# An RWKV-7 scan with two hops a chunk in place of three, in a hybrid decoder layer on one Trainium2 core

## The reference, cut to what matters

```
def step(s, inp):
    r_t, w_t, k_t, v_t, a_t, b_t = inp
    sa = jnp.einsum('bhij,bhj->bhi', s, a_t)
    s = s * w_t[:, :, None, :] + sa[..., None] * b_t[:, :, None, :] + v_t[..., None] * k_t[:, :, None, :]
    return s, jnp.einsum('bhij,bhj->bhi', s, r_t)
```

## Time and profile before

| | us |
|---|---|
| median of 3 runs | 4218.8 (4216.9 to 4219.01) |
| the profiled execution's own time | 4218.97 |
| its span | 4217.2 |
| TensorE busy | 3944.5 (94%) |
| VectorE busy | 2359.7 (56%) |
| ScalarE busy | 1541.6 (37%) |

### The profile page before, as it was taken

How to read it: one execution, slowest core, us unless ns; L and a number is a source line. 1 busy time by engine, 2 the same in 40 slices (tenths; PEclk the granted TensorE clock), 3 DMA queues, 4 the chain that set the end, 5 groups by cost and what they waited for, 6 DMA issues and landing times. The chain is left out here.

```text
span 4217.2 us, 85220 instructions
## 1 busy us (share of the span) xinstructions
PE 3944.5 (94%) x36213; PEld 3629.2 (86%) x36213; DVE 2359.7 (56%) x4632; ACT 1541.6 (37%) x2869; POOL 154.7 (4%) x152
## 2 busy tenths in 40 slices
PE   8999999999989999889978999969989899999998
PEld 4889999999988888889977777769869889999997
DVE  4445656332278886348877777545632464444446
ACT  3113232231177554334326666534411441111112
POOL 0000000000001111010000000000011000000000
PEclk9999999999999999999989999989998999999999
DMA  5323223233355554555641111042323031111112
GB/s 209 83 90 93 90 89 98 80 97 113 114 148 144 147 163 134 168 152 176 215 159 35 42 34 35 21 169 98 103 80 114 27 110 46 48 43 49 42 31 83
DMA packets 375321, 418.74 MB, mean 99 GB/s; under 512 B 50250, under 2 KB 317052, under 8 KB 374076
## 3 DMA queue, kind: packets, MB, share of 16 engines
q1 hardware_dynamic: 362703, 368.14, 28.6%
q0 software_dynamic: 7632, 27.84, 2.2%
q10 hardware_dynamic: 4608, 17.30, 1.0%
HBM read 289.10 MB, written 121.77 MB: 97 GB/s over the span
## 5 line engine op out<-in xcount | busy, mean ns | idle before, releaser
L245 PE MATMUL bank<-xn_hi,pw_whi 128*128 128x352 f32 (+1 forms) x2184 | 735.4, 337 | 20.6 <-PEq L54 8.8
L245 PE MATMUL bank<-xn_hi,pw_wlo 128*128 128x352 f32 (+1 forms) x2184 | 711.7, 326 | 0.0
L245 PE MATMUL bank<-xn_lo,pw_whi 128*128 128x352 f32 (+1 forms) x2184 | 711.3, 326 | 0.0
L245 PEld LDWEIGHTS bank<-xn_hi,pw_whi 128*128 128x128 f32 (+1 forms) x2184 | 417.1, 191 | 38.8 <-issue 24.2
L245 PEld LDWEIGHTS bank<-xn_lo,pw_whi 128*128 128x128 f32 (+1 forms) x2184 | 418.4, 192 | 3.3 <-issue 2.2
L245 PEld LDWEIGHTS bank<-xn_hi,pw_wlo 128*128 128x128 f32 (+1 forms) x2184 | 416.9, 191 | 1.3
L258 ACT ACTIVATE ring<-bank 128x352 f32<-128x352 f32 (+1 forms) x273 | 125.8, 462 | 505.5 <-PE bank L245 505.0
L3147 PE MATMUL bank<-bx_hi,bp_whi 128*128 128x384 f32 (+1 forms) x768 | 274.7, 358 | 28.2 <-DVE bx_lo L3208 17.1
L1789 PE MATMUL bank<-sum_x_hi,pw_whi 128*128 128x352 f32 x768 | 255.0, 332 | 39.5 <-DVE sum_x_lo L1768 23.9
L3772 PE MATMUL bank<-bx_hi,bp_whi 128*128 128x384 f32 (+1 forms) x768 | 251.2, 327 | 4.7 <-issue 4.7
L3772 PE MATMUL bank<-ml_hidden_hi,bp_whi 128*128 128x384 f32 (+1 forms) x768 | 254.5, 331 | 0.0
(11 more groups left out here) (693 smaller groups left out, 10366.1 us busy)
## 6 DMA issues: line engine op xcount, KB each, us to landing
ring<-in_w_in_dram SPq DMA_DIRECT2D x90, 512.0 KB, 5.0
proj_scratch<-ring SPq DMA_DIRECT2D x66, 528.0 KB, 2.9
m_seg<-acum_scratch SPq DMA_DIRECT2D x32, 512.0 KB, 6.7
ring<-in_mlp_w_dram SPq DMA_DIRECT2D x16, 1024.0 KB, 5.5
ring<-in_mlp_w_dram SPq DMA_DIRECT2D x32, 512.0 KB, 3.4
gates_scratch<-ring SPq DMA_DIRECT2D x24, 528.0 KB, 4.5
merged_scratch<-sum_gate ACTq DMA_DIRECT2D x24, 528.0 KB, 5.0
m_raw<-proj_scratch SPq DMA_DIRECT2D x24, 512.0 KB, 5.8
```

Source lines behind the costliest of these rows:

```text
L245: last = self.nc.tensor.matmul(ps[0:n, 0:m], w[:, q, 0:n], self.pair[x][:, q, t0:t0 + m], start=q == 0 and j == 0, stop=q == KD - 1 and j ...
```

## The change

`Invert` gets a twelfth step, "through", in slots 23 and 24, and three steps get more to do. In cross1, TensorE also turns A's rows (AR·eye), and ScalarE copies them into A2. In cross2 it also makes KX·V (with `swapped`), and ScalarE writes that in the place of KX. In through it multiplies A2 with N, and ScalarE writes N·A in the place of A. `Scan` then has U = N (KX V) + (N A) S as one sum of two products in bank 0: VectorE copies it into U in slot 3c (L1485 of the changed kernel), and B·U follows in slot 3c+1, with ScalarE's copy into ST (L1493). Slot 3c+2 has nothing of the scan. R, its semaphores and ScalarE's copy into U are gone, and N·KX of the next chunk starts bank 0 in place of KX·V.

```diff
--- before.py
+++ after.py
@@ -1110,7 +1110,7 @@
 HEADS = (slice(0, 64), slice(64, 128))
 
 INVERSION = [("gram", "v"), ("rows_kb", "a"), ("rows_vd", "a"), ("square", "va"), ("fourth", "va"), ("eighth", "va"), ("by8", "v"),
-             ("turn", "va"), ("cross1", "v"), ("cross2", "v"), ("cross3", "v")]
+             ("turn", "va"), ("cross1", "va"), ("cross2", "va"), ("cross3", "v"), ("through", "a")]
 STEPS = {p + (0 if s == 0 else 2 * s + 1): (s, p) for s in range(len(INVERSION)) for p in range(2)}
 EACH = {w: sum(w in who for _, who in INVERSION) for w in "va"}
 
@@ -1327,9 +1327,16 @@
             elif step == "turn":
                 heads(mm, b0[:, q], x.O[:, i, :], x.X[:, i, :], start=True, stop=True)
                 last = heads(mm, b1[:, q], x.X[:, i, :], v.eye, start=True, stop=True)
+            elif step == "cross1":
+                heads(mm, b0[:, q], x.F[:, i, :], x.G[:, i, :], start=True, stop=True)
+                last = heads(mm, b1[:, q], AR[:, 0:RC], v.eye, start=True, stop=True)
+            elif step == "cross2":
+                heads(mm, b1[:, q], x.F[:, i, :], v.N[:, w, c, :], start=True, stop=True)
+                last = swapped(mm, b0[:, q], v.KX[:, w, c, 0:RC], V, start=True, stop=True)
+            elif step == "cross3":
+                last = heads(mm, b0[:, q], x.F[:, i, :], v.N[:, w, c, :], start=True, stop=True)
             else:
-                y = x.G[:, i, :] if step == "cross1" else v.N[:, w, c, :]
-                last = heads(mm, (b1 if step == "cross2" else b0)[:, q], x.F[:, i, :], y, start=True, stop=True)
+                last = heads(mm, b1[:, q], x.A2[:, i, :], v.N[:, w, c, :], start=True, stop=True)
         last.then_inc(self.pes[p], 1)
 
     def vector(self, dve, r, slot, read):
@@ -1394,8 +1401,14 @@
             last = copy(x.A4[:, :, :], b1)
         elif step == "eighth":
             last = copy(x.A8[:, :, :], b1)
+        elif step == "turn":
+            last = copy(x.G[:, :, :], b1)
+        elif step == "cross1":
+            last = copy(x.A2[:, :, :], b1)
+        elif step == "cross2":
+            last = copy(v.KX[:, r % 2, c, 0:RC], b0)
         else:
-            last = copy(x.G[:, :, :], b1)
+            last = copy(v.AR[:, r % 3, c, 0:RC], b1)
         last.then_inc(self.as_[p], 1)
 
 
@@ -1405,10 +1418,9 @@
     def __init__(self, k, v):
         self.k, self.v, self.nc = k, v, k.nc
         S = lambda n: k.sem(f"rs_{n}")
-        self.r_mm, self.r_off, self.u_mm, self.u_off, self.s_mm, self.s_off, self.read = (
-            S("r_mm"), S("r_off"), S("u_mm"), S("u_off"), S("s_mm"), S("s_off"), S("read"))
+        self.u_mm, self.u_off, self.s_mm, self.s_off, self.read = S("u_mm"), S("u_off"), S("s_mm"), S("s_off"), S("read")
         self.y_off, self.turned, self.t_off, self.out = S("y_off"), S("turned"), S("t_off"), S("out")
-        self.kx_mm, self.vk_mm, self.st_mm, self.kv_mm = S("kx_mm"), S("vk_mm"), S("st_mm"), S("kv_mm")
+        self.vk_mm, self.st_mm, self.kv_mm = S("vk_mm"), S("st_mm"), S("kv_mm")
 
     def updates(self, r, c):
 
@@ -1436,18 +1448,17 @@
                     if r:
                         pe.wait_ge(self.y_off, r)
                 if n % 16 == 0:
-                    swapped(mm, both[:, 0:RC], KX[:, 0:RC], V, start=True, stop=True).then_inc(self.r_mm, 1)
+                    heads(mm, both[:, 0:RC], N, KX[:, 0:RC], start=True, stop=True).then_inc(self.u_mm, 1)
                 else:
                     if c == 0:
-                        swapped(mm, both[:, 0:RC], KX[:, 0:RC], V, start=True, stop=False).then_inc(self.kx_mm, 1)
+                        heads(mm, both[:, 0:RC], N, KX[:, 0:RC], start=True, stop=False)
                     pe.wait_ge(self.s_off, self.updates(r, c))
-                    pe.wait_ge(self.kx_mm, self.carried(n))
-                    heads(mm, both[:, 0:RC], AR[:, 0:RC], ST, start=False, stop=True).then_inc(self.r_mm, 1)
+                    heads(mm, both[:, 0:RC], AR[:, 0:RC], ST, start=False, stop=True).then_inc(self.u_mm, 1)
                     heads(mm, state[:, 0:RC], v.eye, ST, start=True, stop=False).then_inc(self.st_mm, 1)
+                if c:
+                    pe.wait_ge(self.read, n)
                 swapped(mm, o, V, KX[:, RC:2 * RC], start=True, stop=False).then_inc(self.vk_mm, 1)
             elif sub == 1:
-                pe.wait_ge(self.r_off, n + 1)
-                heads(mm, both[:, 0:RC], N, v.R, start=True, stop=True).then_inc(self.u_mm, 1)
                 pe.wait_ge(self.vk_mm, n + 1)
                 if n % 16:
                     heads(mm, o, ST, AR[:, RC:2 * RC], start=False, stop=False)
@@ -1455,13 +1466,12 @@
                 elif r:
                     pe.wait_ge(self.t_off, r // 2)
                 swapped(mm, state[:, 0:RC], K, V, start=n % 16 == 0, stop=False).then_inc(self.kv_mm, 1)
-            else:
                 pe.wait_ge(self.u_off, n + 1)
                 pe.wait_ge(self.kv_mm, n + 1)
                 heads(mm, state[:, 0:RC], B, v.U, start=False, stop=True).then_inc(self.s_mm, 1)
                 heads(mm, o, v.U, BR, start=False, stop=True).then_inc(self.read, 1)
                 if c < 7:
-                    swapped(mm, both[:, 0:RC], v.KX[:, w, c + 1, 0:RC], v.V[:, z, c + 1, :], start=True, stop=False).then_inc(self.kx_mm, 1)
+                    heads(mm, both[:, 0:RC], v.N[:, w, c + 1, :], v.KX[:, w, c + 1, 0:RC], start=True, stop=False)
         elif slot == 24 and w:
             pe.wait_ge(self.s_off, self.updates(r, 8))
             heads(mm, state[:, 0:RC], v.ST[:, 0, :], v.eye, start=True, stop=True).then_inc(self.turned, 1)
@@ -1471,17 +1481,14 @@
             return
         v, c, sub = self.v, slot // 3, slot % 3
         if c < 8 and sub == 0:
-            dve.wait_ge(self.r_mm, 8 * r + c + 1)
-            self.nc.vector.tensor_copy(v.R[:, :], self.k.bank[0][:, 0:RC]).then_inc(self.r_off, 1)
+            dve.wait_ge(self.u_mm, 8 * r + c + 1)
+            self.nc.vector.tensor_copy(v.U[:, :], self.k.bank[0][:, 0:RC]).then_inc(self.u_off, 1)
 
     def scalar(self, act, r, slot, stored):
         if not 0 <= r < ROUNDS:
             return
         v, c, sub = self.v, slot // 3, slot % 3
         if c < 8 and sub == 1:
-            act.wait_ge(self.u_mm, 8 * r + c + 1)
-            self.nc.scalar.activation(v.U[:, :], self.k.bank[0][:, 0:RC], ACT.Copy).then_inc(self.u_off, 1)
-        elif c < 8 and sub == 2:
             act.wait_ge(self.s_mm, 8 * r + c + 1)
             self.nc.scalar.activation(v.ST[:, (c + 1) % 2, :], self.k.bank[1][:, 0:RC], ACT.Copy, scale=v.PC[:, r % 3, c:c + 1]).then_inc(self.s_off, 1)
         elif slot == 24:
@@ -2238,7 +2245,7 @@
         v.F = [r0[:, 3072:3584], r0[:, 3584:4096]]
         v.KX = r1[:, 0:2048].rearrange("p (w c n) -> p w c n", w=2, n=2 * RC)
         v.y = r1[:, 3072:4096].rearrange("p (w t) -> p w t", w=2)
-        v.PC, v.ST, v.R, v.U, v.SO = sb("PC", [P, 3, 8]), sb("ST", [P, 2, RC]), sb("R", [P, RC]), sb("U", [P, RC]), sb("SO", [P, RC])
+        v.PC, v.ST, v.U, v.SO = sb("PC", [P, 3, 8]), sb("ST", [P, 2, RC]), sb("U", [P, RC]), sb("SO", [P, RC])
         v.ex = sb("ex", [P, 8, 1 + RC])
         v.bonus, v.raw, v.pm = sb("bonus", [P, 4, RW]), sb("raw", [P, 3, 1 + RW]), sb("pm", [P, 2, RW])
         work = sb("work", [P, 8, RW])
```

## The result

The changed kernel takes **4264.71 us** (median of 4 runs, 4263.17 to 4272.96); the kernel before, run beside it on the same chip, 4218.91 (4216.9 to 4220.39). The ratio is 1.0113, interval 1.0095 to 1.013: slower by 46 us, where 4213 had been forecast and 4226 was the range's upper end. The profiled execution took 4264.38.

A forecast was written before the change was run, and what follows sets the result against it. ACT's queue was taken to pace a steady round's first half, TensorE the second. Steady rounds −0.7, round without preparation −0.2, tail −5.7, prologue +1.0 sum to −5.6 against 4218.97: 4213 us, range 4203 to 4226.

The forecast's parts named there:

- In the scan* R·N goes (8 × 0.115) and N·KX comes [...] 0: TensorE's scan issue in a steady round: six `heads` a chunk before and after, so no added cost, 0.
- ST is now made one slot earlier and has two inversion steps over it: Scan hops in a steady round: two inversion steps cover ST's hop, and U has the one that R had.
- round without preparation: The round with no inversion beside the scan: waits of 2.0 us go against 1.84 added, gain 0.2.
- tail: The last scan running alone, nothing covering a hop: without the R hop a gain of 5.7 us, bounds 4 and 7.
- case 3: Rival, chance 0.10 including other slower risks: KX·V in cross2 isn't hidden, 0.92 us a round is paid, 4228.
- Steady round: Full rounds with scan and inversion: gain and loss of 0.83 cancel; 0.1 gained in every second round, 0.7 us in all.
- First half: Steady round from the gram's first pass to the second half of step "fourth", paced by ACT: gain 0.83 us.
- ST's (0.20) moves to where ACT waits for TensorE anyway: ScalarE's queue between K's copy and L1209: ST's copy costs nothing there, the stretch shrinking from 2.29 to 1.92 us.
- second half: Rest of the steady round, 17.03 us, paced by TensorE: 1.84 added less covered waits, loss 0.83 us.
- Case 1: Rival, chance 0.31: all TensorE's waits are gained and ACT's queue gives way, 0.66 us a round, 4205.
- Case 2: Rival, chance 0.13: ACT's added 0.6 us a round is paid in full, 8.4 lost less 4.9 at both ends, 4222.
- A tail chunk that stays near 2 us: Sign of a wrong forecast, in the last scan: the second hop would cost more than its rows.

The follow-up runs named there:

- kv_first: The changed kernel with K·V issued earlier, in slot 3c, a whole slot ahead of the wait for it, and eye·ST moved to slot 3c+1: 4223.0 us, ratio 1.0002.
- prework_products: The kernel before plus the inversion's added products (AR·eye, KX·V, A2·N), results unread, without ScalarE's six added copies a round: 4238.0 us, ratio 1.0053.
- prework_only: The kernel before plus the changed kernel's inversion steps, added products and copies, results unread, scan still with three hops: 4247.8 us, ratio 1.0063.
- filled: The changed kernel with two independent products, ST·BR and the next N·KX, issued between K·V and the wait for it: 4240.9 us, ratio 1.0051.
- last_round_only: The kernel before, with the two-hop scan, K·V issued early, and its prepared products and copies for the last round alone: 4214.4 us, ratio 0.9988.
- kv_first_wait_same: The changed kernel with K·V issued early, plus an unneeded wait of V·KX for K·V on the same quadrants: 4253.8 us, ratio 1.0089.

## Why the prediction was wrong, by its own steps

**The step that failed** is "*In the scan* R·N goes (8 × 0.115) and N·KX comes [...] 0", with the one on hops, "ST is now made one slot earlier and has two inversion steps over it". They follow the semaphores from one engine to another and price products by issue alone. They don't ask what else the slot covered. K·V's wait had its cover in the slot that goes; the earlier trace rows show no such wait because it was covered. Seven bare waits of this kind did stand in the waits view of before, for KX·V at the first chunk of every second round:

```profile
PE bank L1125 <- PE bank L1132: 1.1, 7, 0.2
```

and TensorE's timeline has the price at each of them:

```profile
2665.71 0.22 PE L1132 MATMUL bank<-r_V,ring 64*64 64x64 f32 x1
2666.09 0.24 PE L1125 MATMUL bank<-r_ST,r_AR 64*64 64x64 f32 x1 [0.16 <-PE bank L1132]
```

From start to start that is 0.38, so 0.32 of lost issue by the forecast's own way of counting (less 0.06), and 8 × 0.32 = 2.6 a round is what came. The missing term is what the changed kernel's windows have over kv_first's: 2.58 in each of thirteen rounds (33.5), 0.8 in the first scan round (32.3 for 31.5), 2.3 in the round without preparation, 5.6 in the tail. That is 42.2; their medians differ by 41.7. In the tail the wait is some 2.6 (8 × 0.33) and the rest the lower clock that came with it, 0.74 for 1.00. No rival had it: case 3's 4228 was for another mechanism.

**The rest of the sum** can be read from kv_first, where that wait is covered; the sum was −5.6, and the medians say +2.2 (interval −3 to +5).
- *Steady round, forecast even or −0.1.* Measured +0.33, 4.3 us in thirteen. (The round that the forecast followed took 31.64, its counterpart below 32.20.) First half, in the round from T = 2640.69 of this timeline of ScalarE in kv_first:

```profile
2641.17 0.60 ACT L1503 ACTIVATE ring<-bank 128x512 f32<-128x512 f32 x1
...
2643.70 0.69 ACT L1203 ACTIVATE r_work<-bank,vec 128x512 f32<-128x512 f32 x1
...
2645.71 0.68 ACT L1206 ACTIVATE r_work<-bank,vec 128x512 f32<-128x512 f32 x1
2646.28 0.39 ACT L1390 ACTIVATE r_K<-bank 128x256 f32<-128x256 f32 x1
...
2647.34 0.36 ACT L1493 ACTIVATE r_ST<-bank,r_PC 128x64 f32<-128x64 f32 x1
...
2648.38 0.72 ACT L1209 ACTIVATE r_work<-r_pm,vec 128x512 f32<-128x512 f32 x1
```

  y's copy at T+0.48, the sigmoid at T+3.01, the second at T+5.02, K's copy at T+5.59: forecast 0.48, 2.99, 5.01, 5.59. Then L1209 at T+7.69, not 7.51. "ST's (0.20) moves to where ACT waits for TensorE anyway" was wrong: the row at 2647.34 still stands in the way. (The step has a slip too: 2.29 less 0.13 and 0.20 is 1.96, not 1.92.) "Fourth" starts at T+14.14, not 13.78, so the gain is 0.47 and not **0.83**. The second half takes 18.06 for 17.03, a loss of 1.03 and not **0.83**.
- *The first scan round* was taken for a steady one. It took 29.0 before and takes 31.5 in kv_first: +2.5. Kernels with the added products alone have most of it or all: 31.4 in prework_products, 30.8 in prework_only. Nothing of Finish shares this round; that the products are less covered for this reason was not tested.
- *The round without preparation:* −0.2 forecast, +0.9 measured. Its waits did not cover the added products: they cost 2.8 there in prework_products, more than the 1.84 of their issue.
- *The tail:* −5.7 forecast, −1.7 in the changed kernel, −7.3 in kv_first. The mechanism was right and was hidden by the missed wait and by the clock. VectorE's copies of U there stand 1.51 apart, where R's were 2.06 apart in the earlier trace rows:

```profile
2735.73 0.23 DVE L1485 COPY r_U<-bank 128x64 f32<-128x64 f32 x1 [1.37 <-PE bank L1126]
2737.23 0.23 DVE L1485 COPY r_U<-bank 128x64 f32<-128x64 f32 x1 [1.27 <-PE bank L1126]
2738.74 0.23 DVE L1485 COPY r_U<-bank 128x64 f32<-128x64 f32 x1 [1.28 <-PE bank L1126]
```

  That is 0.55 a chunk for the 0.66 forecast. The rest is the clock, below.
- *The prologue:* +1.0 forecast; from the stage's first sigmoid to the scan's first copy +1.2 in the changed kernel, +0.2 in kv_first.

**The rivals.** Case 1 falls: ScalarE was in the way as said, and the waits for its L1209 rose from 3.0 us to 7.7 in kv_first and 9.1 in the changed kernel. Case 2's 4222 is near kv_first's 4223, but mostly by luck: the copies are 0.39 a round, where it had 0.6, and the products' 1.17, which it took as covered, are the larger part. So the warning of the Trainium skill, "TensorEngine Tiling (Array Packing)", section PSUM Bottleneck, holds for a quarter of the added work's price (0.39 of 1.56), and not for the round. Case 3 is refuted by prework_products, whose half of cross2 takes 0.47.

**The signs named.** No wait for ST at chunk 3, through's copies before y's, larger waits for L1209 and A2: all there in the changed kernel. A round of 31.5 to 32.2 and a tail of 15 to 16: neither. "A tail chunk that stays near 2 us" had been named as a sign of being wrong, and it was 1.84 to 1.98 at first, but with another cause than the one written beside it.

## What to carry to other kernels

When a slot is taken out of an interleaved order, list every wait between the two pieces that become neighbours, the waits of an engine for itself first. A covered wait has no row in the profile, so its price has to be taken from one of its kind that is bare, however small its total. Where such a wait must stay, issue its product earlier or put independent products between; that is worth more here than the hop. And a hop pays where nothing covers it, which here was one round of sixteen.

## What the runs showed of the hardware that had not been expected

- A wait of TensorE for the product it has just issued costs 0.22 us of issue between two products on the same quadrants (heads) or 0.26 (swapped), and 0.32 to 0.33 where the quadrants change, against 0.115 for a product. Of the 0.32 to 0.35 only 0.16 to 0.21 is drawn as idle, and the straight wait has no idle drawn ahead of its product at all. What the part that comes with the change of quadrants is, was not settled.
- The granted clock of the tail depends on the version: 0.76 in the kernel before, 0.74 in the changed one, 0.56 in prework_only, and 1.00, the 2.4 GHz level throughout, in kv_first and filled. A short tail alone does not keep it: last_round_only has 0.89 over 15.4 us, and kv_first_wait_same 1.00 over 16.5. What decides it was not settled. The windows of before show the fall inside the tail, the first two chunks at full clock, then a mean between its two levels, 1.2 and 2.4 GHz:

```profile
2726.90:2731.03 4.13, 2.71 (x77) 1.87 (x72) 0.46 (x3) 1.08 (x4) 0.00 (x0) 1.00 0.19 67
2731.03:2748.00 16.97, 13.74 (x218) 8.71 (x214) 3.19 (x9) 5.43 (x18) 0.00 (x0) 0.70 0.01 2
```

  A chunk took 2.06 in the first and 2.58 in the second. So of kv_first's 7.3 us some 4.4 are the hop (8 × 0.55), and the rest fits the clock that stayed, 0.52 for each chunk behind the second. The forecast had scaled the gain to the lower clock and had not allowed for the clock itself to come back.
